# Joining the stages of a two-layer backbone in pairs: merge with output projection, the two halves of the FFN

## The chip, the core and the metric

The kernel runs on one core of a Trainium2 chip. The metric is the device time of one execution in microseconds, taken as the median of several executions. The core has five engines that run side by side: PE (TensorE, matrix products), ACT (ScalarE), DVE (VectorE), POOL (GpSimd) and SP (SyncE, which only issues transfers here). They are tied to each other by semaphores alone.

## What is computed

A backbone of two layers over 256 context tokens and 256 latent tokens, width 1024. Each layer:

```
hx = modulate(rms_norm(x, g_norm1), mod[0], mod[1])
z_rwkv, z_mla, z_fno, z_gate = split(hx @ w_in)
a = rwkv(z_rwkv) @ w_rwkv_o;  b = attention(z_mla) @ w_mla_o;  f = fourier(z_fno) @ w_fno
g = sigmoid(z_gate).reshape(3, 1024)
x = x + mod[2] * ((g[0]*a + g[1]*b + g[2]*f) @ w_out)          # merge, output projection
h = modulate(rms_norm(x, g_norm2), mod[3], mod[4])
gate, up = split(h @ w_ffn_in)                                  # 1024 x 5632
x = x + mod[5] * ((silu(gate) * up) @ w_ffn_out)                # 2816 x 1024
```

`mod` is `silu(c) @ w_mod + b_mod`, six vectors of 1024 for each layer and each of the two kinds of tokens. In the last layer (layer 1) only the 256 latent tokens are wanted behind the mixers. All is in float32.

## The kernel before

**Stages.** The kernel is one Python function that writes, for each layer, a row of stages: norm, projection, features, scan, attention, Fourier, `merge`, `project_out`, `norm`, `ffn_in`, `ffn_out`. Each stage is a block with one instruction list for each engine. At the end of a block all five engines meet at a barrier, and each goes on with a branch to the next block. `Signal` is a semaphore with a running base: `product(k)` is the k-th mark in the present stage, and `Signal.end_stage()` moves all bases.

**Products.** The activations stand with features on the 128 partitions and tokens along the free dimension: 512 columns in layer 0 (`n = TOK - t0`), 256 in layer 1. A float32 product is done as three products of halves, high and low parts, by `product3` (lines 366 to 368). So an output tile of 128 features over 1024 inputs is 8 x 3 = 24 matrix instructions, and a PSUM bank (`BANK[:, m]`, eight of them) holds it.

**Weights.** SP loads 1 MB pieces into a ring of three slots (`RING`, `Loads`). A piece is cut into chunks. ACT writes a chunk's high part (`make_high`, line 327) and DVE its low part (`make_low`, line 330) to one of three chunk slots, by `c % CHUNKS`. `used(c)` names the product after which chunk c's slot is free. `high_ahead` and `low_ahead` make the first three chunks of the next stage; the next stage is told so by `early`, and then PE doesn't wait for them, since the barrier lies between.

**merge.** Twelve steps (four pairs of output tiles, three branches): PE makes two gate tiles and two branch tiles, ACT the sigmoid, DVE the multiply, POOL the add to a total. After the third branch ACT and DVE write the sum's high and low part (`MERGE`). The last part of PE's list begins the output projection: tile 0, with 6 of its 8 pieces (`OUT_EARLY`), 18 products to bank 0. ACT and DVE make chunks 0 and 1 of `w_out` at the last step, and chunk 2 at the very end.

**project_out.** Eight output tiles, tile m in bank m, from one chunk each. DVE adds each tile to the stream X.

**ffn_in.** 22 pairs of tiles (`FT`), gate and up, in banks 0 to 3 by turns. For each pair u: ACT does the silu of the gate tile (`gate_ready`), DVE multiplies by the up tile (`scaled`), ACT copies the high part (`merged`), DVE subtracts for the low part (`evacuated`). Behind the last pair ACT and DVE make three chunks of `w_ffn_out`.

**ffn_out.** Two halves of four output tiles, each over 11 chunks (2 x 128 rows of the hidden width by 512 columns, so 2 x 4 x 3 = 24 products a chunk). In layer 0, a `Modulation` session runs beside it: 24 pieces of 1 MB of the next layer's `w_mod` come over SP into three slots that lie on the norm's output (`H0`), and PE multiplies one or two behind each chunk (line 439); POOL clears a padding and loads small vectors.

Of the kernel before, what the change touches and what calls it, by code (L numbers as in the profile page):

```python
# [26 lines left out]
P = 128  # L27
D = 1024
DT = D // P
# [111 lines left out]
class Signal:  # L141
# [5 lines left out]
    def __init__(self, ctx, nc, name):  # L147
        self.sem = ctx.enter_context(nc.semaphore(name))
        self.base = 0
        self.made = 0  # L150
        Signal.every.append(self)
# [12 lines left out]

    @staticmethod
    def end_stage():
        for s in Signal.every:
            s.base += s.made
            s.made = 0
# [10 lines left out]
def build_in(ctx, nc, ins, out):  # L180
# [117 lines left out]
    class Chunks:  # L298
# [4 lines left out]
        def __init__(self, sources, chunks, used):  # L303
# [4 lines left out]
            self.early = 0  # L308

# [3 lines left out]
        def issue(self, sp, ahead=None):  # L313
            last = {load: c for c, (load, *_) in enumerate(self.chunks)}
            self.loads.issue(sp, lambda i: low_ready(last[i] + 1 - self.early) if last[i] >= self.early else None, ahead)
# [27 lines left out]
        def arrived(self, pe, c):  # L343
            if c >= self.early:
                pe.wait_ge(*low_ready(c + 1 - self.early))
            return self.part(0, c), self.part(1, c)

        def high_ahead(self, act, before=None):  # L350
            for c in range(CHUNKS):
                if before:
                    n = len(before.chunks)
                    act.wait_ge(*before.used(max(q for q in range(n) if q % CHUNKS == c)))
                self.make_high(act, c)

        def low_ahead(self, dve, before=None):
            done = len(before.chunks) - before.early if before else 0
            for c in range(CHUNKS):
# [36 lines left out]
    def stage():  # L396
        return nc.Block()
# [1503 lines left out]
    def fourier(l, t0, w, ahead):  # L1901
        n = TOK - t0
        tiles = list(range(t0 // P, 4))
        with stage() as block:
# [39 lines left out]
            def _(act):  # L1944
# [6 lines left out]
                for m in range(PAIRS):  # L1951
# [4 lines left out]
                    if m < CHUNKS:  # L1956
                        act.wait_ge(*w.used(max(q for q in range(PAIRS) if q % CHUNKS == m)))
                        ahead.make_high(act, m)
# [36 lines left out]
    OUT_EARLY = DT - 2  # L1995

    def merge(l, t0, w, ahead):
        n = TOK - t0
        branch = (O_R, O_M, O_F)
# [5 lines left out]
        with stage() as block:  # L2005
# [5 lines left out]
            def _(pe):  # L2011
# [107 lines left out]
    def project_out(l, t0, w, ahead):  # L2119
# [280 lines left out]
```

## Time and profile before

| | us |
|---|---|
| median of the runs (3) | 2192.7 |
| lowest and highest run | 2192.47, 2199.86 |
| span of the profiled execution | 2192.6 |
| PE busy in it | 1952.2 (89%) |
| DVE busy | 1039.9 (47%) |
| ACT busy | 754.5 (34%) |
| 16 DMA engines, all loads | 203.96 MB, mean 93 GB/s |

The span runs from the first instruction to the last, and there are 0.1 us between it and the median. The profile is one execution. A page names the costliest groups of instructions; what stands between stages is found in the timeline of an engine, where idle time and what released the engine are put in brackets behind a row. "PEq" is PE's sequencer: PE was released by its own instruction list going on, as after a barrier. The windows view gives, for any stretch, each engine's busy time with the count of its instructions, and the clock that PE was granted as a share of 2.4 GHz.

### The profile page before, as it was taken

The numbers are of one execution on the slowest core, as the hardware profiler recorded it, in microseconds if no ns is written. First come the engines' busy times: TensorE is split into PE (matmuls) and PEld (weight loads), VectorE is DVE, ScalarE is ACT, GpSimd is POOL, SyncE is SP. The second block draws the span as 40 slices with busy tenths as digits, with TensorE's granted clock in tenths as the row PEclk, the third lists the DMA queues.
The fourth block names the chain that finished last, engine by engine and source line by source line (L and its number), as shares of the span: only waits on it lengthen the run. The fifth ranks groups of instructions, "written<-read, shape, count | busy, mean of one in ns | idle before, by whom it ended". The sixth has DMA issues, their size and how long they took to land. (4 is left out here: it accounts for less than half of the span.)

```text
span 2192.6 us, 51555 instructions
## 1 busy us (share of the span) xinstructions
PE 1952.2 (89%) x22829; PEld 1569.6 (72%) x22829; DVE 1039.9 (47%) x1721; ACT 754.5 (34%) x1380; POOL 298.3 (14%) x381
## 2 busy tenths in 40 slices
PE   4985888898899999899998998968888899998988
PEld 1662878753578887688886766737876458998988
DVE  1536666572733333433332216476665363545544
ACT  1334333224632322332221114353332453435432
POOL 2103333202000111100001001043331120100000
PEclk7997999999999999999999998979999999999999
DMA  8513000020113333133236742000001114554543
GB/s 326 188 49 115 5 4 4 4 72 1 39 61 97 90 102 106 39 115 110 83 115 238 286 163 60 28 1 4 5 5 44 32 39 145 177 172 144 176 152 125
DMA packets 143452, 203.96 MB, mean 93 GB/s; under 512 B 6718, under 2 KB 123672, under 8 KB 137088
## 3 DMA queue, kind: packets, MB, share of 16 engines
q1 hardware_dynamic: 141728, 198.96, 27.1%
q8 instruction: 181, 2.97, 0.6%
q0 software_dynamic: 1504, 1.71, 0.2%
q14 instruction: 39, 0.32, 0.1%
HBM read 199.61 MB, written 1.05 MB: 92 GB/s over the span
## 5 line engine op out<-in xcount | busy, mean ns | idle before, releaser
L330 DVE TENSOR_TENSOR W_low<-RING,W_high 128x1024 fp32r<-128x1024 f32 x268 | 329.2, 1232 | 464.2 <-ACT W_high L327 463.9
L366 PE MATMUL BANK<-H_high,W_high 128*128 128x512 f32 (+2 forms) x1472 | 520.2, 353 | 19.2 <-ACT H_high L632 8.9
L368 PE MATMUL BANK<-H_high,W_low 128*128 128x512 f32 (+2 forms) x1472 | 515.5, 350 | 0.0
L367 PE MATMUL BANK<-H_low,W_high 128*128 128x512 f32 (+2 forms) x1472 | 515.4, 350 | 0.0
L327 ACT ACTIVATE W_high<-RING 128x1024 fp32r<-128x1024 f32 x268 | 281.1, 1052 | 598.2 <-PE BANK L368 576.8
L366 PEld LDWEIGHTS BANK<-H_high,W_high 128*128 128x128 f32 (+1 forms) x1472 | 280.5, 191 | 67.4 <-issue 26.4
L367 PEld LDWEIGHTS BANK<-H_low,W_high 128*128 128x128 f32 (+1 forms) x1472 | 280.8, 191 | 36.8 <-issue 0.9
L368 PEld LDWEIGHTS BANK<-H_high,W_low 128*128 128x128 f32 (+1 forms) x1472 | 280.2, 190 | 37.3
L1259 PE MATMUL BANK<-RING,WORK 64*64 64x64 f32 x4352 | 162.6, 222 | 13.8 <-issue 7.9
L1259 PEld LDWEIGHTS BANK<-RING,WORK 64*64 64x64 f32 x4352 | 144.7, 134 | 26.7 <-issue 9.8
L1259 PE MATMUL BANK<-RING 64*64 64x64 f32 (+1 forms) x3840 | 101.5, 255 | 43.9 <-DVE RING L1165 30.2
L366 PE MATMUL BANK<-hidden_high,W_high 128*128 128x512 f32 (+1 forms) x352 | 123.1, 350 | 12.0 <-PEq L2165 12.0
L1259 PEld LDWEIGHTS BANK<-RING 64*64 64x64 f32 x3840 | 94.8, 152 | 49.2 <-issue 47.0
L367 PE MATMUL BANK<-hidden_low,W_high 128*128 128x512 f32 (+1 forms) x352 | 120.6, 343 | 0.0
L368 PE MATMUL BANK<-hidden_high,W_low 128*128 128x512 f32 (+1 forms) x352 | 120.3, 342 | 0.0
L1200 DVE TENSOR_TENSOR RING<-RING,BANK 128x512 f32<-128x512 f32 x128 | 83.4, 683 | 57.4 <-PE BANK L1259 55.2
L1259 PE MATMUL BANK<-WORK,RING 64*64 64x64 f32 x2560 | 103.7, 227 | 7.7 <-issue 4.9
L1119 ACT ACTIVATE WORK<-BANK 128x256 f32<-128x256 f32 (+1 forms) x160 | 57.7, 362 | 117.0 <-PE BANK L1259 101.9
L1259 PEld LDWEIGHTS BANK<-WORK,RING 64*64 64x64 f32 x2560 | 89.0, 138 | 11.1 <-issue 6.9
L2103 POOL TENSOR_TENSOR merge_tiles<-merge_tiles 128x512 f32<-128x512 f32 (+1 forms) x32 | 33.8, 1066 | 447.3 <-DVE merge_tiles L2084 447.3
L366 PEld LDWEIGHTS BANK<-hidden_high,W_high 128*128 128x128 f32 x352 | 68.7, 195 | 34.3 <-issue 27.7
L1072 POOL TENSOR_TENSOR WORK<-vec_rows,masks 128x256 f32<-128x256 f32 x80 | 60.8, 761 | 228.2 <-ACT vec_rows L1113 135.2
(307 smaller groups left out, 2824.9 us busy)
## 6 DMA issues: line engine op xcount, KB each, us to landing
RING<-w_in_dram SPq DMA_DIRECT2D x46, 1024.0 KB, 5.4
RING<-w_ffn_in_dram SPq DMA_DIRECT2D x44, 1024.0 KB, 5.2
lation_weights_ffn<-w_mod_dram SPq DMA_DIRECT2D x24, 1024.0 KB, 6.2
RING<-w_ffn_out_dram SPq DMA_DIRECT2D x20, 1024.0 KB, 5.1
tion_weights_opening<-w_mod_dram SPq DMA_DIRECT2D x8, 1024.0 KB, 8.5
ulation_weights_norm<-w_mod_dram SPq DMA_DIRECT2D x8, 1024.0 KB, 7.0
on_weights_features<-w_mod_dram SPq DMA_DIRECT2D x8, 1024.0 KB, 5.0
RING<-w_out_dram SPq DMA_DIRECT2D x8, 1024.0 KB, 5.2
```

What stands on the lines that cost most here:

```text
L327: high_ready.mark(nc.scalar.activation(self.part(0, c), self.raw(c), ACT.Copy))
L330: low_ready.mark(nc.vector.tensor_tensor(self.part(1, c), self.raw(c), self.part(0, c).bitcast(FP32), ALU.subtract))
L366: nc.tensor.matmul(out, w[0], x[0], start=start, stop=False)
L367: nc.tensor.matmul(out, w[0], x[1], start=False, stop=False)
L368: return nc.tensor.matmul(out, w[1], x[0], start=False, stop=stop)
L1072: s_lm[d].mark(nc.gpsimd.tensor_tensor(LM[d], LTS[d], lanes(level_mask(d, l)), ALU.mult))
L1119: s_x1_out[d].mark(nc.scalar.activation(X1[d][:, :, cols], pairs(4 * d + B_L, 0)[:, :, cols], ACT.Copy))
L1200: s_t[d].mark(nc.vector.tensor_tensor(T2[d].rearrange("p q j t -> p q (j t)"), T2[d].rearrange("p q j t -> p q (j t)"), BANK[:, 4 * d + B_ ...
L1259: last[x] = nc.tensor.matmul(BANK[to[h], bank, at + j * width:at + (j + 1) * width], lhs(j)[rows[h]], rhs(j)[rows[h]], start=start and (j ...
L2103: pool_sig.mark(nc.gpsimd.tensor_tensor(total(m), total(m), gate(u), ALU.add))
```

## The change

1. `merge` and `project_out` share one block, and so do `ffn_in` and `ffn_out`. There is no barrier between the two parts, only a branch.
2. Chunk slots turn: `follow` sets a stage's first slot to the one that comes free first, so chunks 0, 1, 2 of the next stage follow the last three chunks of this one in order.
3. In a joined stage (`joined`) PE and SP wait for the low part of every chunk, the ones made ahead too (`split`). Loads that were issued freely behind the barrier now wait for the chunk.
4. `merge` begins two output tiles early, each with 18 products, in banks 0 and 1. `project_out` ends both before it goes on to tile 2, and waits for the pieces of the sum, and for banks 2 and 3, by `before`, which counts marks of the stage ahead.
5. `ffn_in` makes chunk 0 of `w_ffn_out` at the beginning of the last pair and chunk 1 behind its gate; chunk 2 stays behind the last copy.
6. `ffn_out` writes its first half to banks 4 to 7 and its second to 0 to 3 (they were the other way round). The session's banks change with them: (0, 1, 4) and 5 for (4, 5, 0) and 1. PE waits for each piece of the hidden activations in the first half. SP's first modulation load and POOL's list wait for the last product of `ffn_in`.

```
+        def split(self, c):
+            if c >= self.early or self.joined:
+                return low_ready.sem, low_ready.base + c + 1 - self.early
+            return None
         def part(self, x, c):
-            return WS2[x][:, c % CHUNKS, 0:k * w].rearrange("p (k w) -> p k w", k=k)
+            return WS2[x][:, (c + self.turn) % CHUNKS, 0:k * w].rearrange("p (k w) -> p k w", k=k)
+        def follow(self, before):
+            self.turn = (before.turn + len(before.chunks)) % CHUNKS
+        def frees(self, c):
+            return self.used(len(self.chunks) - CHUNKS + c)
...
-                pe.wait_ge(*low_ready(split + 1))
-                pe.wait_ge(*gate_ready(2 * final + 1))
-                pe.wait_ge(*h_ready(OUT_EARLY))
-                first = [ahead.part(x, 0) for x in range(2)]
-                for k in range(OUT_EARLY):
-                    product3(BANK[:, 0, 0:n], [x[:, k] for x in first], [x[:, k, t0:] for x in MERGE], k == 0, False)
+                for m in range(OUT_TILES):
+                    pe.wait_ge(*low_ready(split + m + 1))
+                    pe.wait_ge(*gate_ready(2 * final + m + 1))
+                    pe.wait_ge(*h_ready(OUT_EARLY))
+                    wm = [ahead.part(x, m) for x in range(2)]
+                    for k in range(OUT_EARLY):
+                        product3(BANK[:, m, 0:n], [x[:, k] for x in wm], [x[:, k, t0:] for x in MERGE], k == 0, False)
...
                     wm = w.arrived(pe, m)
-                    for k in range(OUT_EARLY if m == 0 else 0, DT):
+                    if m in (2, 3):
+                        pe.wait_ge(*scaled.before(2 * len(steps) + m - 3))
+                    for k in range(OUT_EARLY if m < OUT_TILES else 0, DT):
+                        if m == 0:
+                            pe.wait_ge(*h_ready.before(k + 1))
...
                 for u in range(FT):
+                    if u == FT - 1:
+                        ahead.high_ahead(act, w, 0, 1)
                     act.wait_ge(*pe_sig(u + 1))
...
                     w.high(act, 2 * u + 1 + CHUNKS)
+                    if u == FT - 1:
+                        ahead.high_ahead(act, w, 1, 2)
                     act.wait_ge(*scaled(u + 1))
                     merged.mark(nc.scalar.activation(HID[0][:, u, t0:], tile(u), ACT.Copy))
-                ahead.high_ahead(act, w)
+                ahead.high_ahead(act, w, 2, CHUNKS)
...
+        bank = lambda x, m: 4 * (1 - x) + m
...
                     w.loads.start(sp, SLOTS)
+                    sp.wait_ge(*product.before(FT))
                     for i in range(MOD_SLOTS):
                         session.load(sp, i)
...
+                        if x == 0:
+                            pe.wait_ge(*evacuated.before(k + 1))
+                        if x == 1 and k == 0:
+                            pe.wait_ge(*scaled.before(FT))
...
-        merge(l, t0, w_merge, w_out)
         w_ffn_in, w_ffn_out = ffn_in_weights(l), ffn_out_weights(l)
-        project_out(l, t0, w_out, w_ffn_in)
+        with stage() as block:
+            merge(l, t0, w_merge, w_out, block)
+            project_out(l, t0, w_out, w_ffn_in, block)
...
+        with stage() as block:
+            ffn_in(l, t0, w_ffn_in, w_ffn_out, block)
+            ffn_out(l, t0, w_ffn_out, session, w_next, block)
```

The order of instructions, with the semaphores that each waits for, shows the change at three places. Lines of the new file stand some 20 to 40 further down: lines 366 to 368 became 387 to 389, line 327 became 341.

PE at the end of `ffn_in` in layer 0, before (`H_` are the norm's output, `hidden_` the activations between the halves):

```order
L367 MATMUL BANK<-H_low,W_high 128x512
L368 MATMUL BANK<-H_high,W_low 128x512
L2165 UNCONDITIONAL_BRANCH
L2267 UNCONDITIONAL_BRANCH [waits barrier_Pool_Activation_PE_DVE_SP_release]
L366 MATMUL BANK<-hidden_high,W_high 128x512
L367 MATMUL BANK<-hidden_low,W_high 128x512
L368 MATMUL BANK<-hidden_high,W_low 128x512
```

and now:

```order
L388 MATMUL BANK<-H_low,W_high 128x512
L389 MATMUL BANK<-H_high,W_low 128x512
L2309 UNCONDITIONAL_BRANCH
L387 MATMUL BANK<-hidden_high,W_high 128x512 [waits evacuated,weights_low]
L388 MATMUL BANK<-hidden_low,W_high 128x512
L389 MATMUL BANK<-hidden_high,W_low 128x512
```

The barrier is gone and one branch is left; the first product of `ffn_out` waits for its own weights and its own piece of the activations.

ACT in the last pair of `ffn_in`, layer 0, before (`W_high<-RING` is a chunk's high part, `ffn_tiles` the silu, `hidden_high` the copy):

```order
L2197 ACTIVATE hidden_high<-ffn_tiles 128x512 [waits scaled]
L2194 ACTIVATE ffn_tiles<-BANK 128x512 [waits evacuated,pe_step]
L2197 ACTIVATE hidden_high<-ffn_tiles 128x512 [waits scaled]
L327 ACTIVATE W_high<-RING 128x1024 [waits slot_full_0,pe_step]
L327 ACTIVATE W_high<-RING 128x1024 [waits slot_full_0,product]
L327 ACTIVATE W_high<-RING 128x1024 [waits slot_full_1,product]
L2165 UNCONDITIONAL_BRANCH
L2296 UNCONDITIONAL_BRANCH [waits barrier_Pool_Activation_PE_DVE_SP_release]
L469 ACTIVATE condition_padded_ffn<-silu_c 128x8x2 [waits padding_cleared]
```

and now:

```order
L2227 ACTIVATE ffn_tiles<-BANK 128x512 [waits evacuated]
L2232 ACTIVATE hidden_high<-ffn_tiles 128x512 [waits scaled]
L341 ACTIVATE W_high<-RING 128x1024 [waits slot_full_0,product]
L2227 ACTIVATE ffn_tiles<-BANK 128x512 [waits evacuated,pe_step]
L341 ACTIVATE W_high<-RING 128x1024 [waits slot_full_0,pe_step]
L2232 ACTIVATE hidden_high<-ffn_tiles 128x512 [waits scaled]
L341 ACTIVATE W_high<-RING 128x1024 [waits slot_full_1,product]
L2345 UNCONDITIONAL_BRANCH
L491 ACTIVATE condition_padded_ffn<-silu_c 128x8x2 [waits padding_cleared]
```

Two of the three high parts moved: one ahead of the last silu, one ahead of the last copy. On DVE the low parts moved in the same way, ahead of the last multiply.

PE between `merge` and `project_out` in layer 0, before (`merge_` is the sum of the branches):

```order
L367 MATMUL BANK<-merge_low,W_high 128x512
L368 MATMUL BANK<-merge_high,W_low 128x512
L2005 UNCONDITIONAL_BRANCH
L2126 UNCONDITIONAL_BRANCH [waits barrier_Pool_Activation_PE_DVE_SP_release]
L366 MATMUL BANK<-merge_high,W_high 128x512
```

and now, with the rest of each run of 18 products left out:

```order
L388 MATMUL BANK<-merge_low,W_high 128x512
L389 MATMUL BANK<-merge_high,W_low 128x512
L387 MATMUL BANK<-merge_high,W_high 128x512 [waits h_ready,gate_ready,weights_low]
L388 MATMUL BANK<-merge_low,W_high 128x512
...
L389 MATMUL BANK<-merge_high,W_low 128x512
L2152 UNCONDITIONAL_BRANCH
L387 MATMUL BANK<-merge_high,W_high 128x512 [waits h_ready,weights_low]
L388 MATMUL BANK<-merge_low,W_high 128x512
L389 MATMUL BANK<-merge_high,W_low 128x512
L387 MATMUL BANK<-merge_high,W_high 128x512 [waits h_ready]
...
L387 MATMUL BANK<-merge_high,W_high 128x512 [waits scaled,weights_low]
```

A second run of early products stands ahead of the join, and five of PE's products behind it wait for the chunk, the piece of the sum or the bank that the barrier stood for.

## Rows read from the trace of the kernel before

**Rows 1.** The first line of the page.

```profile
span 2192.6 us, 51555 instructions
```

**Rows 2.** Timeline of PE at four stops; start us, us, engine, line, operation.

```profile
861.19 0.39 PE L368 MATMUL BANK<-merge_high,W_low 128*128 128x512 f32 x1
863.74 0.47 PE L366 MATMUL BANK<-merge_high,W_high 128*128 128x512 f32 x1 [2.16 <-PEq L2005]
...
1160.25 0.39 PE L368 MATMUL BANK<-H_high,W_low 128*128 128x512 f32 x1
1166.89 0.77 PE L366 MATMUL BANK<-hidden_high,W_high 128*128 128x512 f32 x1 [6.25 <-PEq L2165]
...
1945.24 0.28 PE L368 MATMUL BANK<-merge_high,W_low 128*128 128x256 f32 x1
1948.98 0.35 PE L366 MATMUL BANK<-merge_high,W_high 128*128 128x256 f32 x1 [3.46 <-PEq L2005]
...
2111.68 0.28 PE L368 MATMUL BANK<-H_high,W_low 128*128 128x256 f32 x1
2117.73 0.55 PE L366 MATMUL BANK<-hidden_high,W_high 128*128 128x256 f32 x1 [5.78 <-PEq L2165]
```

**Rows 3.** Windows view; busy us (count) by engine, granted clock, DMA share, GB/s.

```profile
863.74:868.14 4.40, 4.40 (x12) 3.50 (x13) 1.80 (x3) 1.06 (x1) 0.00 (x0) 0.61 0.71 236
868.14:905.10 36.96, 36.93 (x163) 30.22 (x161) 10.46 (x17) 4.24 (x4) 0.00 (x0) 1.00 0.26 86
1166.89:1171.88 4.99, 4.99 (x12) 3.96 (x13) 0.00 (x0) 0.22 (x1) 4.82 (x10) 0.53 0.82 284
1948.98:1953.41 4.43, 4.43 (x24) 4.43 (x25) 1.71 (x2) 1.06 (x1) 0.00 (x0) 0.61 0.70 237
2117.73:2124.10 6.37, 6.37 (x30) 6.37 (x31) 0.00 (x0) 0.87 (x1) 0.00 (x0) 0.52 0.52 166
2124.10:2184.00 59.90, 59.90 (x500) 59.73 (x498) 25.84 (x26) 19.23 (x19) 0.00 (x0) 1.00 0.37 124
```

**Rows 4.** Timelines of ACT and DVE at the ends of both first FFN stages.

```profile
1155.24 0.60 ACT L2194 ACTIVATE ffn_tiles<-BANK 128x512 f32<-128x512 f32 x1 [4.02 <-PE BANK L368]
...
1162.01 2.93 ACT L327 ACTIVATE W_high<-RING 128x1024 fp32r<-128x1024 f32 x3
...
1163.08 3.50 DVE L330 TENSOR_TENSOR W_low<-RING,W_high 128x1024 fp32r<-128x1024 f32 x3 [0.25 <-ACT W_high L327]
...
2109.12 0.38 ACT L2194 ACTIVATE ffn_tiles<-BANK 128x256 f32<-128x256 f32 x1 [1.94 <-PE BANK L368]
...
2113.91 1.22 DVE L330 TENSOR_TENSOR W_low<-RING,W_high 128x1024 fp32r<-128x1024 f32 x1 [0.52 <-ACT W_high L327]
```

**Rows 5.** Timeline of DVE, last low part before layer 1's output projection.

```profile
1947.43 1.22 DVE L330 TENSOR_TENSOR W_low<-RING,W_high 128x1024 fp32r<-128x1024 f32 x1 [0.52 <-ACT W_high L327]
```

**Rows 6.** Timeline of PE, first product behind the norm stage.

```profile
931.90 0.47 PE L366 MATMUL BANK<-H_high,W_high 128*128 128x512 f32 x1 [0.60 <-PEq L615]
```

**Rows 7.** Modulation loads 1, 2, 6: issues, their landing, and PE's use.

```profile
1166.84 1.29 SPq L429 DMA_DIRECT2D lation_weights_ffn<-w_mod_dram  x3
...
lation_weights_ffn<-w_mod_dram SPq DMA_DIRECT2D x1, 1024.0 KB, 5.0
...
lation_weights_ffn<-w_mod_dram SPq DMA_DIRECT2D x1, 1024.0 KB, 7.4
...
1183.38 0.33 SPq L429 DMA_DIRECT2D lation_weights_ffn<-w_mod_dram  x1
...
lation_weights_ffn<-w_mod_dram SPq DMA_DIRECT2D x1, 1024.0 KB, 10.0
...
1195.62 1.92 PE L439 MATMUL BANK<-lation_weights_ffn,condition_padded_ffn 128*32 128x512 f32 x16
```

**Rows 8.** Timeline of PE between two tiles of layer 1's merge stage.

```profile
1862.38 0.28 PE L368 MATMUL BANK<-H_high,W_low 128*128 128x256 f32 x1
1862.50 0.28 PE L366 MATMUL BANK<-o_fourier_high,W_high 128*128 128x256 f32 x1
```

More of the change, by code:

```diff
@@ L15 @@
-from contextlib import ExitStack
+from contextlib import ExitStack, nullcontext
 import concourse.bass as bass
@@ L163, in __call__, with before @@
         return self.sem, self.base + k
+    def before(self, k):
+        return self.sem, self.ahead_of + k
     @staticmethod
@@ L314, in issue @@
             last = {load: c for c, (load, *_) in enumerate(self.chunks)}
-            self.loads.issue(sp, lambda i: low_ready(last[i] + 1 - self.early) if last[i] >= self.early else None, ahead)
+            self.loads.issue(sp, lambda i: self.split(last[i]), ahead)
+        def split(self, c):
+            if c >= self.early or self.joined:
+                return low_ready.sem, low_ready.base + c + 1 - self.early
+            return None
         def raw(self, c):
@@ L394, in build_in, with stage @@
     dft_in = ctx.enter_context(nc.semaphore("dft_in"))
-    def stage():
-        return nc.Block()
+    def stage(block=None):
+        return nc.Block() if block is None else nullcontext(block)
     SUPER, MOD_COLS, MOD_SLOTS = 3, 4 * 512, 3
@@ L1902, in fourier @@
         n = TOK - t0
+        ahead.follow(w)
         tiles = list(range(t0 // P, 4))
@@ L1956, in _ @@
                     if m < CHUNKS:
-                        act.wait_ge(*w.used(max(q for q in range(PAIRS) if q % CHUNKS == m)))
-                        ahead.make_high(act, m)
+                        ahead.high_ahead(act, w, m, m + 1)
             @block.vector
@@ L1993, in merge_weights, with merge @@
         return Chunks(sources, chunks, lambda c: pe_sig(c // 3 * 2 + c % 3 + 1) if c % 3 < 2 else product(c // 3 * 2 + 2))
-    OUT_EARLY = DT - 2
-    def merge(l, t0, w, ahead):
+    OUT_TILES, OUT_EARLY = 2, DT - 2
+    def merge(l, t0, w, ahead, block):
         n = TOK - t0
+        ahead.follow(w)
         branch = (O_R, O_M, O_F)
@@ L2004, in merge @@
         split = len(w.chunks) - w.early
-        with stage() as block:
+        with stage(block) as block:
             @block.sync
@@ L2117, in out_weights, with project_out @@
                       [(m // 2, 0, DT, (m % 2) * P, P) for m in range(DT)], lambda c: product(c + 1))
-    def project_out(l, t0, w, ahead):
+    def project_out(l, t0, w, ahead, block):
         n = TOK - t0
-        with stage() as block:
+        w.joined = True
+        with stage(block) as block:
             @block.sync
@@ L2160, in ffn_in_weights, with ffn_in @@
                       lambda c: (product if c % 2 else pe_sig)(c // 2 + 1))
-    def ffn_in(l, t0, w, ahead):
+    def ffn_in(l, t0, w, ahead, block):
         n = TOK - t0
         tile = lambda u: FTMP[:, u % 2, 0:n]
-        with stage() as block:
+        ahead.follow(w)
+        with stage(block) as block:
             @block.sync
@@ L2229, in ffn_out_weights, with ffn_out @@
         return Chunks(sources, chunks, used)
-    def ffn_out(l, t0, w, session, ahead):
+    def ffn_out(l, t0, w, session, ahead, block):
         n = TOK - t0
+        w.joined = True
+        bank = lambda x, m: 4 * (1 - x) + m
         def multiplied_behind(c):
@@ L2240, in multiplied_behind @@
             return range(*done)
-        with stage() as block:
+        with stage(block) as block:
             @block.sync
@@ L2263, in _ @@
                     for x in range(SLOTS):
[L2264 removed]
+                        sp.wait_ge(*w.split(last[len(w.sources) - SLOTS + x]))
                         ahead.loads.start(sp, x + 1)
@@ L2328, in _ @@
                 if session:
+                    pool.wait_ge(*product.before(FT))
                     pad_condition(pool, session)
```

49 lines of the change are left out of this document (27 added, 22 removed).

## The prediction

> **What bounds the kernel now.** The page's first part comes first: the span is 2192.6 us [rows 1], and the runs' median is 2192.7, so the sum below is made against the span and carried over unchanged. Everything the change touches is TensorE (PE) work that feeds itself: in the steady half of the last stage 500 products of 256 columns start in 59.90 us, 0.120 us apart, at granted clock 1.00; those of 512 columns start 36.96/163 = 0.227 us apart [rows 3]. There PE is the bound and the makers of its weights (ScalarE for the high parts, VectorE for the low parts) have slack. What is not PE work is read from PE's own timeline at the stage ends: four stops whose releaser is PE's sequencer at the end of a block, two behind the merge stage and two behind the first FFN stage [rows 2]. Last, the windows view tells the clock that PE got after each stop: 0.61, 0.53, 0.61 and 0.52, that is mostly the lower of its two levels (1.2 GHz, not 2.4) once PE has stood idle, and 1.00 again after [rows 3].
>
> **The price of the four stops.** From the last start before a stop to the first after it, less one spacing [rows 2]: merge of layer 0, 863.74 - 861.19 - 0.23 = 2.32 us; first FFN stage of layer 0, 1166.89 - 1160.25 - 0.23 = 6.41; merge of layer 1, 1948.98 - 1945.24 - 0.12 = 3.62; first FFN stage of layer 1, 2117.73 - 2111.68 - 0.12 = 5.93. Together 18.3 us. The slow stretches behind them, at their length less what the same products take at full clock [rows 3]: 4.40 - 12 x 0.227 = 1.7; 4.99 - 12 x 0.227 = 2.3; 4.43 - 24 x 0.12 = 1.6; 6.37 - 30 x 0.12 = 2.8. Together 8.3 us. So 26.6 us hang on the four places: 4.0, 8.7, 5.2 and 8.7.
>
> **Do the FFN stops go?** The stop is there because three chunks of the next stage's weights are made after the last product: ScalarE 2.93 us for three high parts, VectorE 3.50 us for three low parts, then a barrier [rows 4]. The change makes chunks 0 and 1 earlier: their slots are free after the products of the tile before the last and after the last gate product, since the ring of slots is now turned. In layer 0, chunk 1 is the later one: gate activation from 1155.24 to 1155.8, high part 1.0, low part 1.2, ready at about 1158.1; the last products start at 1160.25. Chunk 0 stands ahead of it. The raw weights of both were asked for when the chunks of earlier tiles were made, and the order of those is untouched. Chunk 2 keeps its place behind the last product, the multiply and the copy, where the first of the three is today: high part from 1162.01, low part from 1163.08, ready at 1164.3 [rows 4]. PE wants it after two chunks of 24 products, 1160.48 + 10.9 + 1.0 for one modulation load = 1172.4. In layer 1 its low part runs from 2113.91 to 2115.1 [rows 4], so the chain from the last product's start takes 3.4 us, and it is wanted at 2111.80 + 48 x 0.12 = 2117.6. So 2.5 us of slack, and both stops go. Chunk 3 waits for chunk 0's use and then for 1.0 + 1.2 us, with two chunks (5.8 us) of PE work in front of it. The output banks don't collide either: the first half now writes banks 4 to 7, which the stage before doesn't use.
>
> **Do the merge stops go?** PE stops there since chunk 2 of the output projection is made last and the barrier waits for it: in layer 1 its low part runs from 1947.43 to 1948.65 [rows 5], and PE starts at 1948.98; in layer 0 it is made by 863.74, when PE starts [rows 2]. Behind the last early product there are now 30 products before that chunk is wanted: 18 of the second tile, 12 that finish both tiles. Layer 0: 861.42 + 30 x 0.227 = 868.2, over 4 us after it is made. Layer 1: 1945.36 + 30 x 0.12 = 1948.95, only 0.3 us after it is made. Both go, the second with next to no margin; a miss there costs tenths, not the stop.
>
> **What the change adds.** (a) A branch stays at each join on each engine. The trace of before has no branch without a barrier. Upper bound: where PE itself was the last to arrive at a barrier, two branches and the barrier cost a gap of 0.60 [rows 6]; lower bound 0, if PE's queue covers it. Nearest is the FFN stop, where 0.31 us pass from the end of VectorE's last low part (1166.58) to PE's first product, a barrier and one branch [rows 2, 4]. I take 0.15 each, 0.6 together, and keep 0 to 2.4. (b) Some 54 more waits on PE's products, nearly all long satisfied. A product with a satisfied wait follows its neighbour at the usual 0.12 us [rows 8]: nothing. (c) In layer 0 the modulation loads are asked for at the last product, some 1160.8, instead of 1166.84 [rows 7], which is 6.0 us earlier, while PE's need for them comes 8.7 us earlier (6.4 and 2.3). So every slack in this queue shrinks by 2.7 us. The first load lands 5.0 us after its issue, at 1165.8; PE comes to it at 1160.48 + 24 x 0.227 + 0.1 = 1166.0. The tightest of the later ones is the sixth: issued at 1183.38, landed 10.0 later at 1193.4, wanted at 1195.62 + 0.96 = 1196.6 [rows 7]; 3.2 us of slack become 0.5, if the queue stays full and so can't deliver sooner. Bounds 0 to 2.7 us; I take 0.3, as both margins come out positive. (d) On VectorE two low parts now stand ahead of the last multiply, and on ScalarE two high parts ahead of the last copy. Chunk 1's low part ends at 1158.1, before the products do. In layer 1 it ends at 2109.12 + 0.38 + 1.0 + 1.2 + some 0.1 = 2111.8 [rows 4], just as the last product starts. Nothing. (e) The banks, the turned slots in the Fourier and merge stages, and the wait on GpSimd change no order that PE sees.
>
> **The sum.** 26.6 - 0.6 - 0.3 = 25.7 us; 2192.7 - 25.7 = **2167.0 us**, 1.2% less. By the bounds of (a) and (c), with a tenth or two for layer 1's chunk 2, it is 2166 to 2171.
>
> **A rule that speaks against it.** At the barrier behind the norm stage PE is itself last and is through two branches and the barrier in 0.60 us [rows 6], so no instruction fetch is seen to hold it there. The Trainium skill, Runtime: NRT & Kernel Launch, Instruction fetch mechanics, says that a taken branch whose target isn't in the pages held has to fetch that page by DMA before the engine goes on. By that rule a join could stop where, before, the fetch lay under the idle time. The same skill's Advanced Engine Details and Errata, Control Flow Timing, gives a plain branch some 51 ns: by that, an estimate, the joins would cost 0.2 us and not 0.6, and the time would be 2166.6.
>
> **Rivals.**
> 1. A join stops PE for a fetch. The nearest price of a round trip to memory is a load's 5.0 us [rows 7], and a stop of that size brought a slow stretch of 2.3 [rows 2, 3]. At one join of the four: 2167 + 7.3 = 2174. For it: the branch is still there and no idle time covers it. Against: the 0.60 at a barrier with PE last.
> 2. The modulation loads come late. If the first one lands like the second, 7.4 us after issue [rows 7], PE stops 2.2 us, as long as the stop at 861.58, which was followed by a slow stretch; 2.2 + 2.3 = 4.5, so 2171.5. For it: the margins of 0.2 and 0.5 us. Against: the change sends no other transfer ahead of the first.
> 3. The FFN stops only move to chunk 2 or 3, since two slots run ahead and not three. Then layer 1's 8.7 and layer 0's 8.7 are given back: 2184.4. It decides from the point where the chain from the last product's start grows from 3.4 to over 5.9 us in layer 1. The rows leave 2.5 us.
> 4. Slower than before: the waits on nearly every second group of products keep PE from loading ahead. If each of the 54 cost what PE pays at a barrier it reaches last, 0.60 + 0.16 of lost overlap = 0.76 [rows 6], that is 41 us: 2167 + 41 = 2208. It ends above 2192.7 from 0.48 us a wait on. Against it stands [rows 8], where a waiting product loses nothing.
>
> **Chances.** Forecast 0.76 (its own range 2165 to 2170), rival 1 0.06, rival 2 0.10, rival 3 0.05, rival 4 0.02; 0.01 is left for what I don't see. The range takes the forecast, rival 2 and a stop at one join: 2164 to 2174, where 2164 allows 26.6 in full and 2 us of slow stretches elsewhere that fall otherwise. A measurement can tell 0.5%, 11 us, from no change. Faster by more: forecast and rivals 1 and 2, 0.92, plus half of the unseen: 0.93. Within it: rival 3, 0.05. Slower: 0.02.
>
> **What would show it.** In the timeline of PE no idle time over 0.3 us between merge and norm and between norm and the next layer; in the windows view clock 1.00 in both; the first FFN stage's last multiply at its old distance to the last product. Rival 1: a gap right at the join. Rival 2: PE waiting on the modulation's load. Rival 3: PE idle before the third or fourth chunk. Rival 4: spacings over 0.12 us at the products with waits. The forecast is wrong if the slow stretches stay though the stops are gone.

## The result and the profile after

| | kernel before, us | changed kernel, us | ratio (95%) |
|---|---|---|---|
| first comparison | 2193.64 (4 runs) | 2173.55 (4 runs, 2169.53 to 2177.54) | 0.9887 (0.9864 to 0.9911) |
| second comparison | 2196.86 (15 runs) | 2169.75 (5 runs, 2165.18 to 2172.93) | 0.9877 (0.9855 to 0.9899) |

By the ratios the change makes the kernel 1.1 to 1.2% faster, and neither interval comes near 1. The medians differ by 20.1 us in the first comparison and by 27.1 in the second, where 25.7 were forecast. The ratio of the first comparison stands for more than its medians do: 0.9887 of 2193.64 is 24.8 us less, and the quotient of the two medians is 0.9908. Both lie in its interval, 19.5 to 29.8 us. The measured 2173.55 lies in the range of 2164 to 2174, half a microsecond from its upper end, and outside the forecast's own 2165 to 2170. Ratios and intervals here and below use fast runs alone; one slow run of merge_join_alone, 2310.23 us at clock 0.82, is left out of its ratio but not of its median.

The answer to [rows 2] is PE's timeline of the changed kernel at both FFN joins and at the first early tile of layer 1's merge stage (start us, us, engine, line, operation):

```profile
1164.50 0.39 PE L389 MATMUL BANK<-H_high,W_low 128*128 128x512 f32 x1
1164.72 0.39 PE L387 MATMUL BANK<-hidden_high,W_high 128*128 128x512 f32 x1
...
1940.77 0.28 PE L389 MATMUL BANK<-o_fourier_high,W_low 128*128 128x256 f32 x1
1940.89 0.35 PE L387 MATMUL BANK<-merge_high,W_high 128*128 128x256 f32 x1
...
2103.55 0.28 PE L389 MATMUL BANK<-H_high,W_low 128*128 128x256 f32 x1
2103.67 0.28 PE L387 MATMUL BANK<-hidden_high,W_high 128*128 128x256 f32 x1
```

No row has a bracket: across both FFN joins the products stand 0.22 and 0.12 us apart, their usual spacing, where PE had stood idle for 6.25 and 5.78 us. The merge joins lie 36 early products behind the first early tile's start. PE's timeline there, layer 0 and layer 1, where the stops were 2.16 and 3.46 us:

```profile
873.26 0.39 PE L389 MATMUL BANK<-merge_high,W_low 128*128 128x512 f32 x1
873.49 0.39 PE L387 MATMUL BANK<-merge_high,W_high 128*128 128x512 f32 x1
...
1945.15 0.28 PE L389 MATMUL BANK<-merge_high,W_low 128*128 128x256 f32 x1
1945.27 0.28 PE L387 MATMUL BANK<-merge_high,W_high 128*128 128x256 f32 x1
```

They too stand 0.23 and 0.12 us apart. The answer to [rows 3] is the clock (windows view; busy us and count of PE, PEld, DVE, ACT, POOL, then clock, DMA share, GB/s):

```profile
865.33:910.91 45.58, 43.69 (x194) 35.85 (x192) 16.92 (x27) 8.21 (x10) 2.49 (x2) 1.00 0.28 92
936.16:1318.22 382.06, 379.27 (x1754) 294.68 (x1755) 114.87 (x137) 92.57 (x114) 10.02 (x20) 1.00 0.46 159
1940.89:1965.44 24.55, 23.26 (x194) 23.06 (x192) 13.93 (x21) 7.43 (x10) 1.43 (x2) 1.00 0.52 172
1982.65:2168.14 185.49, 184.55 (x1537) 184.37 (x1537) 97.08 (x115) 80.63 (x108) 0.00 (x0) 1.00 0.52 171
```

These are the four places as whole stretches: from the first early product of the output projection to the next norm, and from the first product of the first FFN stage to the next norm or, in layer 1, to the last stage. The clock is 1.00 in all four. The ends of the same stretches in the kernel before are these starts in PE's timeline:

```profile
857.34 0.39 PE L366 MATMUL BANK<-merge_high,W_high 128*128 128x512 f32 x1
...
906.97 0.70 PE L641 MATMUL BANK<-WORK,ones 128*32 128x512 f32 x2 [1.90 <-ACT WORK L621]
...
1322.52 1.06 PE L641 MATMUL BANK<-WORK,ones 128*32 128x512 f32 x1 [1.61 <-ACT WORK L621]
...
1943.13 0.35 PE L366 MATMUL BANK<-merge_high,W_high 128*128 128x256 f32 x1
...
1972.86 0.43 PE L641 MATMUL BANK<-WORK,ones 128*32 128x256 f32 x2 [1.29 <-ACT WORK L621]
...
1990.78 0.35 PE L366 MATMUL BANK<-H_high,W_high 128*128 128x256 f32 x1 [0.60 <-PEq L615]
...
2184.98 0.30 PE L2369 MATMUL BANK<-ident,X 128*128 128x128 f32 x1 [0.94 <-PEq L2242]
```

With 931.90 from [rows 6] they give 49.63, 390.62, 29.73 and 194.20 us, 664.18 together. The table below reads every kernel in the same way. It is the measure used from here on, since it sees only the places and not the rest of the program. before_again and after_again are second profiles of the two programs; the other names are those of the experiments.

| us | merge L0 | FFN L0 | merge L1 | FFN L1 | four places | rest of the span |
|---|---|---|---|---|---|---|
| before | 49.63 | 390.62 | 29.73 | 194.20 | 664.18 | 1528.4 |
| before_again | 49.60 | 390.57 | 29.73 | 192.78 | 662.68 | 1524.6 |
| changed | 45.58 | 382.06 | 24.55 | 185.49 | 637.68 | 1538.0 |
| after_again | 45.58 | 381.90 | 24.55 | 185.48 | 637.51 | 1526.7 |
| ffn_join_alone | 49.78 | 382.45 | 29.88 | 185.47 | 647.58 | 1524.8 |
| merge_join_alone | 45.57 | 391.12 | 24.56 | 193.88 | 655.13 | 1539.8 |
| chunks_early_barrier | 45.58 | 387.82 | 24.54 | 190.76 | 648.70 | 1523.0 |
| chunks_late_join | 45.58 | 388.78 | 24.56 | 190.45 | 649.37 | 1535.2 |
| one_early_tile | 45.58 | 382.10 | 25.90 | 185.49 | 639.07 | 1521.4 |
| two_tiles_barrier | 46.31 | 382.41 | 26.25 | 185.48 | 640.45 | 1515.3 |
| two_tiles_timed | 46.30 | 381.96 | 26.24 | 185.48 | 639.98 | 1521.4 |
| branch_per_chunk | 45.58 | 381.91 | 24.56 | 185.48 | 637.53 | 1523.3 |
| mod_loads_late | 45.58 | 389.31 | 24.54 | 185.47 | 644.90 | 1525.2 |
| slots_not_turned | 45.57 | 382.15 | 24.55 | 185.49 | 637.76 | 1528.8 |

The changed kernel is 26.5 us shorter in the four places: 4.05, 8.56, 5.18 and 8.71. But its profiled span, 2175.7, is only 16.9 below that of before, as the rest is 9.6 us longer. That rest is the first thing to explain. The norm stages that lie between these places take 42.9 and 42.7 us together in the two profiles of before and 42.5 and 42.8 in those of the changed kernel, so the gain is not given back next door.

### The profile page after: what moved, and what is told of

Read it like the earlier page. It is cut to its first block and busy times, and to the rows that moved or that the text cites. A ratio compares the mean times of both kernels' runs of the same rounds, so it can differ in the third digit from the quotient of the medians.

```text
span 2175.7 us, 51544 instructions
## 1 busy us (share of the span) xinstructions
PE 1947.3 (90%) x22829; PEld 1563.0 (72%) x22829; DVE 1041.6 (48%) x1721; ACT 754.9 (35%) x1380; POOL 297.8 (14%) x381
```

## The experiments

### The same two programs once more

No edit. What was expected of the changed kernel:

> The changed kernel once more, nothing left out. Its first profile has the four stops gone and 26.4 us less in the stages of the change, yet it reached the first merge stage at 669.4 us where the kernel before reached it at 661.4, over code that neither program changes. Theory: the stages ahead of the joins differ from run to run by several us in both programs, so this profile has the four places as before within 0.3 us (merge to norm 45.6 in layer 0 and 24.6 in layer 1, first FFN product to the next norm 153.5), its start of the first merge lies anywhere from 660 to 670, and the ratio is 0.988 to 0.990. Rival: the changed program is slower there by itself. Then the first merge starts again at 669 +- 1 and every run is some 7 us above 2167.

and of the kernel before:

> The kernel before once more, for a second profile. Theory of variation from run to run: the first merge product starts somewhere from 660 to 670 us. Rival, that the changed program is slower there: 661 +- 1.

Measured: the places repeat within 0.2 us in the changed kernel, the rest does not: 1526.7 against 1538.0 us for one and the same program. The windows view of its two profiles shows this for the scan of layer 0 and a short stretch behind it, first the changed kernel, then after_again:

```profile
488.99:510.06 21.07, 16.30 (x57) 9.67 (x57) 12.33 (x11) 6.28 (x13) 0.00 (x0) 0.92 0.23 73
217.12:446.85 229.73, 194.72 (x7425) 176.56 (x7425) 142.84 (x284) 74.49 (x218) 72.33 (x95) 0.97 0.02 4
```
```profile
477.25:496.72 19.47, 14.70 (x56) 8.54 (x57) 12.34 (x11) 6.29 (x13) 0.00 (x0) 0.98 0.25 78
216.51:436.64 220.13, 192.37 (x7425) 174.94 (x7425) 143.11 (x284) 74.61 (x218) 72.46 (x95) 0.98 0.02 5
```

The same 7425 instructions of PE take 229.73 us in one and 220.13 in the other, and the kernel before lies between them, at 225.42 and 223.04. The short stretch takes either 21.07 or 19.47, with clock 0.92 or 0.98; in the kernel before it was 21.05 in one profile and 19.48 in the other. The first merge stage, which began at 661.42 us in before and at 669.37 in the changed kernel, began at 657.31 in after_again. That is below the 660 to 670 expected, and far from the 669 by which the changed program would be slower by itself. before_again, with 661.55, fits either idea. So the idea that the changed program slows down other stages fell, and the 9.6 us are no more than one profiled execution of these stages differs by from another. In all 14 profiles the rest lies between 1515 and 1540 us, and one or two profiles of each kernel show no order by program. The intervals of both comparisons hold 26 us.

In the kernel before, a place can differ too: its layer 1 FFN took 192.78, not 194.20. The slow stretch behind that stop, to be compared with the fifth row of [rows 3], in before_again:

```profile
2113.85:2120.22 6.37, 6.37 (x42) 6.37 (x43) 0.83 (x1) 1.06 (x1) 0.00 (x0) 0.77 0.46 166
```

42 products in 6.37 us at clock 0.77, where it was 30 at 0.52: the slow stretch cost 6.37 - 42 x 0.12 = 1.3 us and not 2.8, behind a stop of the same 5.8 us.

### Each join alone

ffn_join_alone keeps merge and output projection in blocks of their own, with one early tile:

```
-    OUT_TILES, OUT_EARLY = 2, DT - 2
+    OUT_TILES, OUT_EARLY = 1, DT - 2
-        with stage() as block:
-            merge(l, t0, w_merge, w_out, block)
-            project_out(l, t0, w_out, w_ffn_in, block)
+        merge(l, t0, w_merge, w_out, None)
+        project_out(l, t0, w_out, w_ffn_in, None)
```

> Only the FFN stages are joined; merge and output projection have their barrier and one early tile as before. Theory: both FFN stops gone and both merge stops there with their slow stretches, so 8.7 + 8.7 = 17.4 us below before in the places of the change, 2175 to 2178, and 9.2 above the changed kernel. Rival, that a join's gain is partly given back elsewhere: less than 14 us below before.

merge_join_alone does the same to the two FFN calls, and makes all three chunks behind the last copy again.

> Only merge and output projection are joined, two early tiles; the FFN stages have their barrier and make their three chunks behind the last copy as before. Theory: 4.0 + 5.2 = 9.2 us below before, 2183 to 2186, with idle times of PE of 6.3 and 5.8 us at the FFN stages and their slow stretches as before. Rival as above: less than 6 us below before.

Measured beside 2196.86: the FFN joins alone 2180.98 us, ratio 0.9926 (0.9900 to 0.9951), which is 16.3 us; the merge joins alone 2189.12, ratio 0.9958 (0.9940 to 0.9976), which is 9.2 us. Both medians lie above the times expected, 2175 to 2178 and 2183 to 2186, as the kernel before stood at 2196.86 here. In the places the gains are 16.6 and 9.1 us. The sum, 25.7, is what both do together to within a microsecond: the two halves don't need each other. Most of what is missing to 26.5 lies in the stops that stay, each some 0.15 us longer than in the kernel before (2.31 and 3.60 us at the merge, 6.40 and 5.92 at the FFN); why is not shown.

### The two halves of the FFN edit

The barrier kept, chunks 0 and 1 early:

```
-        with stage() as block:
-            ffn_in(l, t0, w_ffn_in, w_ffn_out, block)
-            ffn_out(l, t0, w_ffn_out, session, w_next, block)
+        ffn_in(l, t0, w_ffn_in, w_ffn_out, None)
+        ffn_out(l, t0, w_ffn_out, session, w_next, None)
```

> The changed kernel with the barrier back between the FFN stages; two chunks are still made early. Theory: the barrier now waits for chunk 2's low part alone, ready 4.05 us (layer 0) and 3.5 us (layer 1) after the last product's start. PE stops for 4.1 and 3.6 us over a spacing and gets a slow stretch each time, so in the places of the FFN stops it is 12.8 us above the changed kernel and only 4.6 below before. Rival, that the barrier costs little once two of three chunks are early: under 4 us above the changed kernel.

Joined, but all three chunks behind the last copy, where before has them (on VectorE in the same way):

```
-                    if u == FT - 1:
-                        ahead.high_ahead(act, w, 0, 1)
...
-                ahead.high_ahead(act, w, 2, CHUNKS)
+                ahead.high_ahead(act, w, 0, CHUNKS)
```

> The changed kernel with no barrier between the FFN stages but all three chunks made behind the last copy, as before. Theory: PE starts on chunk 0 as soon as its low part is there, 4.0 and 3.4 us late, again with slow stretches: 12 to 13 us above the changed kernel. Rival, that the barrier was the cost and not the chunks: under 4 us above.

PE's timeline at the two FFN joins, first with the barrier kept, then with the chunks late:

```profile
1159.37 0.47 PE L387 MATMUL BANK<-hidden_high,W_high 128*128 128x512 f32 x1 [4.06 <-PEq L2196]
...
2098.09 0.35 PE L387 MATMUL BANK<-hidden_high,W_high 128*128 128x256 f32 x1 [3.58 <-PEq L2196]
```
```profile
1171.88 0.50 PE L387 MATMUL BANK<-hidden_high,W_high 128*128 128x512 f32 x1 [3.72 <-DVE W_low L344]
...
2110.99 0.39 PE L387 MATMUL BANK<-hidden_high,W_high 128*128 128x256 f32 x1 [3.24 <-DVE W_low L344]
```

With the barrier PE is held by its sequencer until chunk 2, which is wanted 48 products later, is made. Without it, PE waits for chunk 0's low part alone. Each stop is 56 to 65% of the old one, and behind each the clock was low, 0.60 to 0.64 in the first 4.2 to 4.5 us. In layer 0 of the kernel with the barrier (windows view, as above):

```profile
1159.37:1163.60 4.23, 4.23 (x12) 3.33 (x13) 0.00 (x0) 0.22 (x1) 4.06 (x9) 0.60 0.81 281
```

clock 0.60, and 4.23 - 12 x 0.227 = 1.5 us lost. Against the changed kernel these two stand 11.0 and 11.7 us higher in the places. That is a little under the 12.8 and the 12 to 13 expected: the stops came as forecast (4.2 and 3.7 us over a spacing with the barrier, for 4.1 and 3.6), but the slow stretches behind the four stops cost 1.5 to 1.8 us and not the 2.3 and 2.8 of before. Of the 17.3 us that both give together, one half alone gives about 6.

### The two halves of the merge edit

One early tile and the join (`OUT_TILES` 1 for 2):

> The changed kernel with one early tile instead of two ahead of the merge join. Chunk 2 is wanted just as late (30 products on), so only the last two pieces of the sum can hold PE. Theory: layer 0 loses 0 to 0.2 us, as piece 8 is ready at 861.94 and wanted at 862.1 in the time of the first trace; layer 1 loses 1.0 to 1.5 us, as pieces 7 and 8 come at 1946.28 and 1946.91 and are wanted at 1945.36 and 1945.7; no slow stretch. Rival: the second tile is what removes the stops, and without it most of the 4.0 and 5.2 us come back.

Two early tiles and the barrier (`merge(..., None)` and `project_out(..., None)`, as above):

> The changed kernel with the barrier back between merge and output projection and two early tiles. Theory: in layer 0 PE comes last to the barrier and loses 0.8 us; in layer 1 it waits for chunk 2's low part and the barrier, 1.4 to 1.5 us; no slow stretches, so 2.2 us above the changed kernel and 7.0 below before. Rival, that the join is what counts: 5 us or more above the changed kernel.

PE's only stops there, first with one tile, then with the barrier:

```profile
1926.71 0.35 PE L387 MATMUL BANK<-merge_high,W_high 128*128 128x256 f32 x1 [0.92 <-DVE merge_low L2113]
```
```profile
858.68 0.47 PE L387 MATMUL BANK<-merge_high,W_high 128*128 128x512 f32 x1 [0.45 <-PEq L2029]
...
1924.35 0.36 PE L387 MATMUL BANK<-merge_high,W_high 128*128 128x256 f32 x1 [1.48 <-PEq L2029]
```

With one tile and the join, layer 0 needs nothing more, and layer 1 waits 0.92 us for the last piece of the sum: 1.35 us in the place. With two tiles and the barrier it is 0.7 and 1.7 us. So either half takes most of the merge places' 9.2 us, and the second tile is worth 1.4 us once the stages are joined. A stop of 1.48 us also brought no slow stretch; the windows view from its end on, two_tiles_barrier:

```profile
1924.35:1928.40 4.05, 4.05 (x34) 4.05 (x35) 2.46 (x4) 2.01 (x2) 0.00 (x0) 1.00 0.76 255
```

34 products in 4.05 us at clock 1.00, against 0.61 behind the 3.46 us of before.

The single times of these two, 2162.34 and 2157.51 us, were the lowest of all, with 2193.98 for the kernel before beside them. By the table that comes from the rest, the shortest seen. The second was timed over more runs:

> Part: the same kernel as two_tiles_barrier (the changed one with the barrier between merge and output projection kept), timed in several rounds, since its single time, 2157.5 us, was the lowest of all. Theory (that time was low by the stages that no program here changes; in the four places it stands 2.8 us above the changed kernel): 26.5 - 2.8 = 23.7 us under the kernel before, so a ratio of 0.989, and its median some 12 to 17 us above that single time if the kernel before is at 2194 to 2197 beside it; its own runs spread over 8 us or more. Rival (the program is better as a whole than the changed kernel, whose ratio was 0.9877): a ratio of 0.984 or less, with all its runs near the single one.

Measured: 2162.68 us (2160.38 to 2166.82) with the kernel before at 2187.41 beside it; ratio 0.9890 (0.9869 to 0.9911), 24.7 us. The forecast ratio was 0.989, and the 0.984 of the rival is outside the interval. Its median is only 5 us above that single time, not 12 to 17, and its runs spread over 6.4 us and not 8; the kernel before stood lower too, on another chip. Only ratios compare between one comparison and another. That the changed kernel is better by the 2.3 to 2.9 us that the places show can't be told from times.

### A branch by itself

PE's list of the second FFN stage cut into a piece for each chunk, 43 branches more:

```
-            @block.tensor
-            def _(pe):
-                for c in range(2 * HALF_CHUNKS):
+            def multiply_chunks(pe, c):
+                for c in (c,):
...
+            for c in range(2 * HALF_CHUNKS):
+                block.tensor(lambda pe, c=c: multiply_chunks(pe, c))
```

> Part: the changed kernel with PE's list for the second FFN stage cut into one piece for each of its 22 chunks, with a branch between two pieces and no barrier: 43 more branches on PE in the two layers, nothing else. Theory (a branch on PE that no barrier goes with lies under the products queued ahead of it): the first product behind each branch starts at the usual spacing, 0.23 us behind the last in layer 0 and 0.12 in layer 1; the FFN places stay at 382.0 and 185.5 us within 0.3 each, the four places at 637.6 within 0.6. The term taken in the prediction, 0.15 us each: +6.5 us in the two FFN places together. The nearest bound from above, 0.60 each: +26 us. Rival (a join can stop PE for a fetch): one or more stops of up to 5.0 us at branches, each with a slow stretch of about 2.3 behind it.

Measured: the four places sum to 637.53 us, against 637.68 and 637.51 without the branches. Two profiles of one kernel differ by as much, so 43 branches cost under 0.2 us together, under 5 ns each. No product of the two second FFN stages' chunks has an idle time before it, so there was no stop for a fetch at any of them. That the products already queued cover the branches is the likely reason; no view shows the queue.

### The margin of the modulation loads

SP's first modulation loads asked for 24 products later:

```
-                    sp.wait_ge(*product.before(FT))
+                    sp.wait_ge(*slot_used(1))
```

> Part: the changed kernel with SP's first modulation loads asked for when the second FFN stage's first chunk has been multiplied, and not at the last product of the first FFN stage: 24 products of 0.227 us, 5.4 us later. Only layer 0 has them. Theory (margin of the changed kernel small but positive, as the prediction has it, 0.2 us; the first load lands 5.0 us behind its issue): PE stops before the first modulation product for 5.2 us and gets a slow stretch of 2 to 2.5 us behind it; later loads are behind by as much in the same queue, so some further stops of up to 0.5 us; the L0 FFN place goes from 382.0 to 387 to 390 us, the other three stay within 0.2. Rival (the loads have several us of slack, as the queue is deep enough): the stop is under 3 us and the place grows by under 4. Rival (the modulation loads were late in the changed kernel already): its own stop is there to be added to, and this one grows by over 5.4 plus a slow stretch.

PE's timeline at the first modulation product, and the windows view behind the stop:

```profile
1166.52 1.94 PE L461 MATMUL BANK<-lation_weights_ffn,condition_padded_ffn 128*32 128x512 f32 x8 [5.01 <-DMA lation_weights_ffn<-w_mod_dram]
```
```profile
1166.52:1172.00 5.48, 5.48 (x19) 3.12 (x20) 0.00 (x0) 0.00 (x0) 0.00 (x0) 0.61 1.00 414
```

A stop of 5.01 us, and the place grew by 7.3 us over the changed kernel's 382.06, so 2.2 to 2.4 us of slow stretch: all of the delay of 5.4 us but some 0.4 reached PE. No later modulation load held PE. The changed kernel has next to no slack here, as the prediction had it, and it is enough.

### The slots not turned

```
-            self.turn = (before.turn + len(before.chunks)) % CHUNKS
+            self.turn = 0
...
-            return self.used(len(self.chunks) - CHUNKS + c)
+            return self.used(max(q for q in range(len(self.chunks)) if q % CHUNKS == c))
```

> Part: the changed kernel without the turning of the chunk slots: a stage's chunk 0 goes to slot 0 again, and each chunk waits for the last user of its slot in the stage ahead. In the first FFN stage, with 44 chunks, chunk 1 of the second then waits for the last product of the last pair; the merge stage's order changes as little. Theory (what removes the FFN stop is the early making of two chunks; turning only says which slot is free first): chunk 0 is made from the slot of the last pair's gate or up chunk and may now come behind the last product. If it does, the multiply and the copy of the last pair, that stand behind chunk 1 on ACT and DVE, come later too: chunk 1's high and low part take 1.0 and 1.2 us, so PE stops at the join in layer 0 for 1 to 3.5 us with a slow stretch behind it, or not at all if only chunk 1 is touched, wanted 24 products (5.4 us) later; in layer 1, 24 products are 2.9 us and the chunks take 3.4, so 0.5 to 2 us. So the two FFN places grow by 0 to 6 us in layer 0 and 0.5 to 4 in layer 1. Rival (turning is worth the whole gain): both places return to 390.6 and 194.2.

Measured: 637.76 us in the places, the same as with turning, so the rival is out. Chunk 1 is now made behind the last product. VectorE's low part of it in layer 1, beside PE's first product of the second stage:

```profile
2094.51 0.28 PE L387 MATMUL BANK<-hidden_high,W_high 128*128 128x256 f32 x1
...
2095.87 1.23 DVE L344 TENSOR_TENSOR W_low<-RING,W_high 128x1024 fp32r<-128x1024 f32 x1 [1.73 <-ACT W_high L341]
```

It is ready at 2097.10 and wanted at 2094.51 + 24 x 0.12 = 2097.39. The chain took 2.7 us from the last product's start and not the 3.4 that was assumed for it, so the cost of 0.5 to 2 us expected for layer 1 did not come. What turning buys is margin, not time: chunk 1 is ready 0.3 us before it is wanted here, and 2.9 us in the changed kernel (2103.66 against 2103.67 + 2.88).

## Why the prediction was right

**The price of the four stops** was right: 26.6 us read from [rows 2] and [rows 3], 26.5 measured between the two profiles (4.05, 8.56, 5.18, 8.71 against 4.0, 8.7, 5.2, 8.7). It was too exact for one term. The slow stretch of 2.8 us in layer 1's FFN was 1.3 in the other profile of the same kernel, so 25 to 26.5 us is what the kernel before pays.

**The FFN stops go**: yes, and by the margins given. The answer to [rows 4], VectorE in the changed kernel, chunks 1 and 2 of layer 0, then of layer 1:

```profile
1161.13 1.22 DVE L344 TENSOR_TENSOR W_low<-RING,W_high 128x1024 fp32r<-128x1024 f32 x1 [3.46 <-ACT W_high L341]
...
1167.26 1.23 DVE L344 TENSOR_TENSOR W_low<-RING,W_high 128x1024 fp32r<-128x1024 f32 x1 [0.26 <-ACT W_high L341]
...
2102.43 1.23 DVE L344 TENSOR_TENSOR W_low<-RING,W_high 128x1024 fp32r<-128x1024 f32 x1 [1.16 <-ACT W_high L341]
...
2105.73 1.23 DVE L344 TENSOR_TENSOR W_low<-RING,W_high 128x1024 fp32r<-128x1024 f32 x1 [0.52 <-ACT W_high L341]
```

In layer 0 chunk 1 is ready at 1162.35 and the last product starts at 1164.50: 2.15 us, as worked out (1158.1 against 1160.25). In layer 1 chunk 2 is ready at 2106.96 and wanted at 2103.67 + 48 x 0.12 = 2109.4: 2.5 us of slack, the figure of the prediction. Rival 3, which needed that chain to grow by 2.5 us, is out.

**The merge stops go**: yes. The answer to [rows 5], VectorE's last low part there in layer 1:

```profile
1945.21 1.23 DVE L344 TENSOR_TENSOR W_low<-RING,W_high 128x1024 fp32r<-128x1024 f32 x1 [0.52 <-ACT W_high L341]
```

Ready at 1946.44, wanted at 1940.89 + 0.07 + 48 x 0.12 = 1946.7: the predicted 0.3 us, without a stop. The two experiments on this edit show how little it hung on: with the barrier kept, the second tile alone took 6.8 us of the 9.2, and the join alone 7.9.

**(a) A branch at each join** was taken at 0.6 us for the four and is nothing that can be read, by the joins themselves (first fence) and by 43 more of them. The step that erred was the choice of the row: the gap of 0.31 us behind a barrier, with PE idle, did not carry over to a branch with products ahead of it; the lower bound was the right end. The Trainium skill, Advanced Engine Details and Errata, Control Flow Timing, gives a plain branch some 51 ns, and the estimate of 0.2 us made from it would have come nearer; under 5 ns a branch, those 51 don't show on PE either. Rival 1, the stop for a fetch, did not come in 47 branches. The rule behind it (Trainium skill, Runtime: NRT & Kernel Launch, Instruction fetch mechanics) asks for a fetch only where the target isn't in the pages held, and whether these were no run here shows.

**(b) The waits** cost nothing, and rival 4 is out: the spacing is unchanged in all four places, which sum to 26.5 us less and not more.

**(c) The modulation loads** were taken at 0.3 us; layer 0's FFN place came out 8.56 and 8.72 us shorter in two profiles, against 8.7 for stop and slow stretch, so 0 to 0.15. The first load is asked for at 1164.91 and lands 4.8 us later; timeline of SP's queue and PE, then the view of the DMAs issued between 1164.8 and 1165.2 us (KB, us to landing):

```profile
1164.91 1.29 SPq L451 DMA_DIRECT2D lation_weights_ffn<-w_mod_dram  x3
...
1170.25 1.06 PE L461 MATMUL BANK<-lation_weights_ffn,condition_padded_ffn 128*32 128x512 f32 x8
```
```profile
lation_weights_ffn<-w_mod_dram SPq DMA_DIRECT2D x1, 1024.0 KB, 4.8
```

At 1169.7, with PE there at 1170.25: 0.5 us of margin for the 0.2 predicted, and mod_loads_late shows that it is real and small. The sixth load, the tightest of the later ones, from the same two views, the DMAs here issued between 1178.6 and 1179.3 us:

```profile
1178.90 0.33 SPq L451 DMA_DIRECT2D lation_weights_ffn<-w_mod_dram  x1
...
lation_weights_ffn<-w_mod_dram SPq DMA_DIRECT2D x1, 1024.0 KB, 12.5
...
1191.15 1.92 PE L461 MATMUL BANK<-lation_weights_ffn,condition_padded_ffn 128*32 128x512 f32 x16
```

It lands at 1191.4 and is wanted at 1191.15 + 0.96 = 1192.1: 0.7 us for the 0.5 predicted. Counted from the last product of the first FFN stage, it was asked for 8.7 us earlier than in [rows 7] (14.4 us behind that product, not 23.1), but took 12.5 us where it took 10.0 there. So 2.5 us of its 3.2 us of slack went, as the prediction had it for a queue that stays full. Rival 2, with a landing after 7.4 us, did not come.

**(e)** held as far as it was tried: with the slots not turned the places stay at 637.76 us. The banks were not varied by themselves; 26.5 us measured for 26.6 leaves them nothing that can be read.

**The transfer to the time** was the loose step. The prediction set the span of 2192.6 beside the median of 2192.7 and saw 0.1 us between them. In the runs that list both, an execution takes 1.8 us more than its span, so the profiled one took about 2194.4 and stood 1.7 above the median. More weighty, the forecast's own range of 2165 to 2170 and the range of 2164 to 2174 were made of the bounds of the sum and, for the wider one, of two rivals, while runs of one program in one comparison here spread over 6 to 17 us and the kernel before came out at 2181.7 to 2196.9 in other comparisons. The miss of 6.5 us against the first comparison's median comes from there and not from the terms: 0.9 us since the kernel before had 2193.64 and not 2192.7 in it, and 5.6 since 20.1 us were measured for the 25.7 forecast, with the places at 26.5. The forecast's own range missed that median. The range of 2164 to 2174 held it, by half a microsecond, thanks to the width given to the rivals, which was not made for this: that much was luck.

## What to carry to other kernels

Price a stage boundary as the stop plus the slow stretch behind it, and look at what the barrier waits for: here it held PE for a chunk that was wanted 48 products later. At the FFN, removing the barrier and making the first chunks early had to come together, as each alone left a 3 to 4 us stop and its slow stretch; at the merge, either half alone took most of the gain. When a saving is near 1%, compare the stretches that the change touches, profile against profile, before believing a difference of medians.

## What was not expected of the hardware

- Stages that both programs share differ from one execution to the next by up to 25 us in 1515 to 1540, much of it in the scan, where the same instructions took 219 to 230 us in layer 0; a short stretch takes 19.47 or 21.07 us, with clock 0.98 or 0.92 in the two profiles of the changed kernel. What decides it no run shows.
- The lower clock followed the stops of 2.16 us and more that were looked at, and neither of 0.92 nor 1.48 us. Behind stops of the same 5.8 us in one and the same program it cost 2.8 us in one profile and 1.3 in another.
- 43 branches on PE between runs of products cost under 5 ns each.
- The sixth modulation load, 1 MB, was asked for 8.7 us earlier, counted from the last product of the first FFN stage, and landed 6.2 us earlier: 12.5 us from issue to landing, and 10.0 before.
